# One DVE instruction, one PSUM bank and one gate product moved in a two-block transformer kernel

## The reference

```
h = h + 0.5*swiglu(rmsnorm(h), w_gu, w_down)          # four times, with a gated positional term twice
# state-space mixer (32 heads of 64, 8 groups, state 128, both directions)
y = y_fwd + y_bwd + xs * d_skip                       # per group g: decay-weighted scores @ xs
y = rmsnorm(y * silu(z), norm_g)                      # mean over 2048 columns: needs the sum of squares
h = h + y @ w_out
# neighbourhood attention, then second block:
q, k, v, ..., f_b, ..., g = split(rmsnorm(x) @ w_in)  # three attentions of 8 heads, one gate of 3 x 1024
o_a = stick_breaking_attention(...)                   # heads 0..7
o_b = forgetting_attention(...)                       # heads 8..15, forget gates from f_b
o_c = moba_attention(...)                             # heads 16..23
mixed = sum_n sigmoid(g_n) * (o_n @ w_branch_n)
x = x + mixed @ w_out;  x = x + relu(rmsnorm(x) @ w_up)**2 @ w_down
return rmsnorm(x)
```

## Time and profile before

| | |
|---|---|
| median of three | 1746.23 us (1744.68 to 1747.62) |
| profiled execution, its own time | 1748.32 us |
| its span, first to last instruction | 1746.5 us |
| mean granted TensorE clock | 0.994 of full |
| busy: PE / PEld / DVE / ACT / POOL | 99 / 83 / 61 / 52 / 7 % |
| data moved | 300.56 MB, mean 172 GB/s; the weight queue takes 52.1% of the 16 DMA engines |

### The profile page before, as it was taken

The page is one execution under the profiler, slowest core; times in us unless marked ns, Lnnn a source line. Parts: engine busy times, 40 slices in busy tenths (PEclk is TensorE's granted clock), DMA queues, the critical chain, the costliest instruction groups (busy, mean ns, idle before and its releaser), DMA issues.

```text
span 1746.5 us, 22965 instructions
## 1 busy us (share of the span) xinstructions
PE 1720.6 (99%) x9356; PEld 1456.6 (83%) x9356; DVE 1066.2 (61%) x1331; ACT 899.7 (52%) x1263; POOL 117.5 (7%) x85
## 2 busy tenths in 40 slices
PE   9999899999999999999999999999999999999998
PEld 7888799998678888888888678888899888888886
DVE  5554478889965545755456856554744555676543
ACT  5443457776754434644355655444643544554532
POOL 0000000000000000000003400000000344100000
PEclk9999899999999999999999999999999999999999
DMA  9554576666456555775454236556465322456551
GB/s 299 182 192 169 149 197 180 193 183 194 132 177 204 180 180 181 190 242 198 170 189 167 78 109 204 183 180 199 150 217 170 121 75 98 144 166 207 176 186 71
DMA packets 243976, 300.56 MB, mean 172 GB/s; under 512 B 9248, under 2 KB 175520, under 8 KB 243872
## 3 DMA queue, kind: packets, MB, share of 16 engines
q1 hardware_dynamic: 238224, 289.25, 52.1%
q10 hardware_dynamic: 5648, 9.85, 2.2%
HBM read 297.96 MB, written 1.11 MB: 171 GB/s over the span
## 4 chain that ended last, share of the span: by engine, by line
PE 93%; DVE 4%; issue 1%; ACT 1%; DMA 0%; ACTq 0%; DVEq 0%; POOL 0%
PE bank L536 90%; PE bank L539 4%; DVE EW L1738 2%; DVE wlo L1738 1%; DMA h<-in_x 0%; DVE Er L1738 0%; ACT whi L1245 0%; DVE yhl L1741 0%; DVE xTs L1741 0%; DVE bc L1741 0%; ACT hThi L1245 0%; DVE xTs L1738 0%; DVE hTlo L1741 0%; ACT yhl L1245 0%; DVE st L2087 0%
## 5 line engine op out<-in xcount | busy, mean ns | idle before, releaser
L1738 DVE TENSOR_TENSOR wlo<-raw,whi 128x2048 fp32r<-128x2048 f32 (+2 forms) x272 | 593.4, 2187 | 341.4 <-ACT whi L1245 341.4
L1245 ACT ACTIVATE whi<-raw 128x2048 fp32r<-128x2048 f32 (+2 forms) x284 | 518.5, 1833 | 263.4 <-PE bank L536 257.8
L536 PE MATMUL bank<-whi,hThi 128*128 128x512 f32 x1072 | 426.0, 397 | 0.0
L536 PE MATMUL bank<-wlo,hThi 128*128 128x512 f32 x1072 | 418.6, 390 | 0.4 <-DVE wlo L1738 0.4
L536 PE MATMUL bank<-whi,hTlo 128*128 128x512 f32 x1072 | 403.3, 391 | 0.0
L536 PE MATMUL bank<-hThi,whi 128*128 128x256 f32 (+1 forms) x912 | 263.2, 289 | 0.8 <-ACT hThi L1245 0.8
L536 PE MATMUL bank<-hTlo,whi 128*128 128x256 f32 (+1 forms) x912 | 259.5, 285 | 0.0
L536 PE MATMUL bank<-hThi,wlo 128*128 128x256 f32 (+1 forms) x912 | 259.3, 284 | 0.0
L536 PEld LDWEIGHTS bank<-whi,hThi 128*128 128x128 f32 x1072 | 201.9, 188 | 43.2 <-issue 3.2
L536 PEld LDWEIGHTS bank<-whi,hTlo 128*128 128x128 f32 x1072 | 201.7, 188 | 43.1 <-DVE hTlo L1741 0.3
L536 PEld LDWEIGHTS bank<-wlo,hThi 128*128 128x128 f32 x1072 | 202.0, 188 | 41.3 <-DVE wlo L1738 1.5
(11 more groups left out here) (205 smaller groups left out, 1962.6 us busy)
## 6 DMA issues: line engine op xcount, KB each, us to landing
raw<-in_ffn_w_gu SPq DMA_DIRECT2D x172, 512.0 KB, 4.9
raw<-in_ffn_w_down SPq DMA_DIRECT2D x40, 1024.0 KB, 5.1
raw<-in_w_in SPq DMA_DIRECT2D x30, 1024.0 KB, 5.2
raw<-in_ssd_w_in SPq DMA_DIRECT2D x16, 1024.0 KB, 5.6
raw<-in_ssd_w_in SPq DMA_DIRECT2D x32, 512.0 KB, 5.5
raw<-in_w_up SPq DMA_DIRECT2D x16, 1024.0 KB, 5.4
raw<-in_w_down SPq DMA_DIRECT2D x16, 1024.0 KB, 5.0
raw<-in_na_w_qkv SPq DMA_DIRECT2D x12, 1024.0 KB, 5.1
```

What stands on the lines that cost most here:

```text
L536: return T.e.matmul(out, lhsT, rhs, start=start, stop=stop, skip_group_check=skip)
L1245: return e.activation(out, in_, ACT.Identity, **kw)
L1738: return e.tensor_tensor(out, a, b, op)
```

## The change

Three edits, none of which adds or removes an instruction.

```
 def three_banks():
-    rot, out = Rot(2, 3, 4, 5, 6, 7), {}
+    rot, out = Rot(3, 4, 5, 6, 7, 2), {}
...
             for g in range(K, 8):
-                if g > K:
-                    squares(g - 2)
                 if g < 7:
                     bounds(g + 1)
                 take("yout", g - 2)
                 if g < 7:
                     products(g + 1)
                 outputs(g)
-                if g == 7:
-                    squares(6)
+                squares(g - 1)
                 columns_of(g)
...
+            def gated(x):
+                V.wait_ge(*at("w_rel", "gate", x))
+                tt(gts[:, 2 * x:2 * x + 2, :], split3(banks[x % 2]), rsb2, ALU.mult).then_inc(*sig("gts", x))
...
                 elif what == "gate":
-                    V.wait_ge(*at("w_rel", "gate", n // 2))
-                    tt(gts[:, n - 1:n + 1, :], split3(banks[n // 2 % 2]), rsb2, ALU.mult).then_inc(*sig("gts", n // 2))
+                    if n < 23:
+                        gated(n // 2)
...
                         done.then_inc(*sig("tfin", n))
+                    if n == 22:
+                        gated(11)
```

## The result

The changed kernel takes 1738.34 us (median of 4 executions, 1735.11 to 1738.78) against 1746.17 us before (1744.68 to 1747.62): ratio 0.995, 95% interval 0.9935 to 0.9965. That is 7.8 us less; 1738.7 was forecast. Run again beside other kernels (`e10_changed`) it took 1739.17 us, ratio 0.9955 (0.9942 to 0.9967).

The account below looks back on a forecast made before the run. PE, busy 99% of the span, was taken as the bound. Waits of 2.0 + 1.9 + 1.5 = 5.4 us plus 3.2 of clock gave 8.6 less: 1739.7 or 1737.6, middle 1738.7 us; range 1735.5 to 1744.0.

Parts of the forecast that it names:

- The first edit's wait: State-space loop: with `ssr` moved behind the gate product, group 7's outputs released 1.98 us earlier; about 1.5 us wait left.
- The split 1.38 + 0.6: State-space loop: 1.38 us from the last swapped sum, 0.6 from the three behind groups 3, 4, 5.
- the view of waits (3.5): PE's three waits for `ssr` total 3.5 us; the gain is only 2.0, since DVE's loop stays the bound.
- The second edit: First scores in bank 3: PE's wait for `fgT` goes, 1.9 us; full clock behind it, 1.50 us more.
- The third: Last gate product behind head 22: PE's wait for `s` goes in full, 1.5 us.
- The clock: Low grant behind two waits goes: 1.68 us at group 7's outputs, 1.50 at first scores and gate half; 3.2 together.
- the slower rival: State-space loop: DVE stops at the moved sum until PE's squares are in, at four places; 3.5 us slower, 1749.7, chance 0.04.
- The sum, 8.6: Whole kernel: 5.4 us of waits (2.0 + 1.9 + 1.5) plus 3.2 us of clock.
- the middle: Whole kernel: 1738.7 us, taken between 1739.7 (from the profiled execution) and 1737.6 (from the median).
- The lower end of the range, 1735.5: Whole kernel: all waits for `ssr` gone, and the median's base 1.5 us lower.

Follow-up runs that it names:

- e10_changed: The changed kernel run again, nothing altered, beside two kernels that build on it (also written e10): 1739.17 us, ratio 0.9955 against the kernel before.
- e8: Kernel before with only the last swap (`squares` ahead of `columns_of` behind group 6): 1742.97 us, ratio 0.9981.
- e2: Kernel before with only the banks' rotation changed, `Rot(3, 4, 5, 6, 7, 2)`: 1743.38 us, ratio 0.9979.
- e1: Kernel before with only the squares edit (DVE part of the diff for `squares`): 1742.4 us, ratio 0.9978.
- e4: Kernel before, two PE waits filled with unread matmuls (19 ahead of group 7's outputs, 15 ahead of the first scores): 1743.05 us, ratio 0.9981.
- e3: Kernel before with only the last gate product, `gated(11)`, moved behind `finish` of head 22: 1745.82 us, ratio 0.9994.
- e5: Changed kernel with each sum of squares one place further ahead, in front of DVE's `outputs(g)`: 1738.31 us, ratio 0.9958 against the kernel before.
- e7: Changed kernel with group 5's squares in bank 5 and 36 unread matmuls ahead of the normalisation's transposes: 1734.14 us, ratio 0.9934 against the kernel before.

## Why the prediction was right

- The first edit's wait: forecast 1.98. From the first `ssr` to the start of group 7's outputs it was 477.58 less 350.9 = 126.7 us before and 474.69 less 349.9 = 124.8 after, 1.9 less. The wait left over was put at about 1.5, and is 1.64. The split 1.38 + 0.6 is borne out by e8.
- That the view of waits (3.5) overstates what such an edit can bring was right: the release came from DVE's own loop, which got only 0.2 shorter per turn, while PE was ready 1.1 earlier, by the two waits of 0.51 that it no longer had.
- The second edit: 1.9 of waiting and 1.5 of clock. The stretch that holds it is 3.4 shorter, and e2 alone gives 3.1.
- The third: 1.5. The stretch is 1.5 shorter; by the total alone it could not have been told. The path to it was read wrong in one step. The prediction had DVE through with head 22's normalisation 2.0 us behind the start of head 23's logits, by the durations before. It took 3.95 (1481.27 to 1485.22), since one instruction of it took 2.38 us beside GpSimd's subtraction. PE wanted the result 1.4 us later still, so the term held by that slack, which by the prediction's numbers was 3.4 (1494.72 less 1491.3); no rival named it, though the row at 1437.05 shows the same in the trace before.
- The clock: 1.68 + 1.50 forecast, and just that in the windows (4.48 to 2.80, 5.41 to 3.91). e1, e2 and e4 each switch one or both on and off. The rule of the Trainium skill (TensorE: Matmul & The Clock Gate, Part 1), by which the point of a change varies from run to run, would have had the falls in some executions only. At these two places the traces speak against a large share: the fall stood behind the 1.9 us wait in all four traces of kernels that have it unfilled (before, e1, e3, e8), behind the 2.4 us wait in all three (before, e2, e3), and behind the waits of 1.0 and 1.6 us for `ssr` in none of six. In the neighbourhood attention five of 13 traces have a fall (before, after, e2, e3, e10), and it goes with no edit there. But each of the two kernels traced twice gave the same both times, so no two traces of one kernel show a fall that comes and goes.
- What was wrong: the price of the slower rival. It counted the same stop four times. e5 builds that stop, and it is paid once, because the engine waited for has the shorter loop.
- The sum, 8.6, was 0.9 under the difference of the two profiled executions (1748.32 less 1738.78 = 9.5); 1.0 of it lies ahead of the first `ssr`, where nothing was changed. It was 0.8 over the difference of the medians, 7.8.
- That 1738.7 came within 0.4 of 1738.34 is in part luck. The median alone would have led to 1737.6 and the profiled execution to 1739.7; the middle was taken for want of a reason for either. The times lie 1735.11 to 1738.78, and the same kernel took 1739.17 when run again. The lower end of the range, 1735.5, also doesn't quite follow from its own two terms: 1738.7 less 1.5 and less 1.5 is 1735.7.

## What to carry to other kernels

On an engine that is 99% busy, a wait of two microseconds can cost nearly as much again in the clock behind it (1.91 and 1.50 us, 2.45 and 1.68 here): price a wait with the window behind it, not with its own length. When two engines loop in step, the gain of an earlier release is bounded by the other's loop, and a stop is paid once and not per turn if the engine waited for has slack. A small instruction in an in-order queue costs nothing inside a wait that exists anyway: look for such a place before looking for less work. But an instruction that is moved can take another time at its new place: look at what the other engines do beside it there, and keep slack for it.

The lowest median is that of the changed kernel with group 5's squares in bank 5 and the 36 unread matmuls (e7), 1734.14 us, 0.9934 of before. By ratio it can't be told from either of the two alone: bank 5 without the unread matmuls is 0.9942 and 0.9933 (1735.38 and 1734.81 us), the unread matmuls without bank 5 are 0.9936.

## What the runs showed of the hardware

- Matmuls that nobody reads kept the clock up: 34 of them shortened the kernel by 3.4 us (e4), with no wait of another engine changed.
- At the places of the three edits, the grant stayed at 1.00 behind every idle stretch of PE of 1.00 to 1.65 us (eleven in all traces), and fell to 0.50 behind every one of 1.91 us (four) and of 2.42 to 2.46 us (three). No run had one between 1.65 and 1.91 us there, and none shows what else a fall needs: in the neighbourhood attention it fell in five of 13 traces, behind idle stretches of 0.8 us or less that all 13 have.
- A DVE instruction of 0.29 us took 2.38 us when it started while GpSimd wrote a `wlo` tile, and ended 0.08 us behind GpSimd's end; reductions beside it kept their length.
- Twice the clock did not halve the stretch behind the long wait: with the 4.4 us wait filled, PE waited 0.6 us longer for ACT behind it.
